# Chunk-causal hybrid encoder layer: GpSimd's head preparation, its low parts in four pieces, an operand on ScalarE

## The reference

```
h  = rmsnorm(x) * (1 + sc1) + sh1
z  = h @ w_in                         # q,k,v | shifted columns | gates
o_a = band attention (8 heads x 64)
o_b = RWKV-7: w_log, a, g, kk from z; S = S*w + sa (kk*a)^T + v k^T; y = S r; group norm; gate
merged = gates_a * (o_a @ w_out_attn) + gates_b * (o_b @ w_out_rwkv)
x  = x + gt1 * (merged @ w_out)       # "output stage" below
h2 = rmsnorm(x) * (1 + sc2) + sh2
x  = x + gt2 * ((silu(gg) * u) @ w_ffn_out),  u, gg = h2 @ w_ffn_in
y  = rmsnorm(x)
```

## Time and profile before

| what | value |
|---|---|
| timed runs | 1097.21 us median, 1095.9 to 1097.24 |
| profiled execution, span from the first to the last instruction | 1095.1 us (its own device time isn't listed apart; the median of the timed runs is 2.1 us above the span) |
| PE, matmuls | 1045.0 us busy (95%) |
| DVE | 395.5 us (36%) |
| ACT | 366.5 us (33%) |
| POOL | 368.7 us (34%) |
| mean granted TensorE clock | 0.980 |
| heads, about | 331 to 535 us |
| attention and RWKV output products, merge | 535 to 620 us |
| output stage | 620 to 674 us |
| feed-forward | 674 to 1085 us |

### The profile page before, as it was taken

The page is one execution under the profiler, slowest core; times in us unless marked ns, Lnnn a source line. Parts: engine busy times, 40 slices in busy tenths (PEclk is TensorE's granted clock), DMA queues, the critical chain, the costliest instruction groups (busy, mean ns, idle before and its releaser), DMA issues.

```text
span 1095.1 us, 25416 instructions
## 1 busy us (share of the span) xinstructions
PE 1045.0 (95%) x10988; PEld 966.9 (88%) x10988; DVE 395.5 (36%) x926; ACT 366.5 (33%) x745; POOL 368.7 (34%) x252
## 2 busy tenths in 40 slices
PE   6999999999998988989898999999999999999997
PEld 3899989999996766777787999999999999999997
DVE  4400000194045676566556576222222222200003
ACT  4443333353444444345232233322322232211112
POOL 2165433343316061401160333333343334344331
PEclk8899999999999999899998999999999999999999
DMA  9986666343311000020341532233222322132322
GB/s 358 352 276 235 234 206 198 99 139 119 113 42 36 18 7 22 13 82 3 131 130 43 198 116 58 77 92 99 77 77 83 107 78 65 55 104 79 92 67 82
DMA packets 118174, 122.23 MB, mean 112 GB/s; under 512 B 5396, under 2 KB 102848, under 8 KB 115656
## 3 DMA queue, kind: packets, MB, share of 16 engines
q1 hardware_dynamic: 112864, 111.86, 31.8%
q10 hardware_dynamic: 5224, 9.10, 2.5%
HBM read 108.33 MB, written 15.23 MB: 113 GB/s over the span
## 4 chain that ended last, share of the span: by engine, by line
PE 86%; DVE 7%; issue 3%; ACT 3%; POOL 1%; ACTq 1%; DVEq 0%; POOLq 0%
PE ps L1566 83%; PE ps L1917 2%; DVE s_sb L1306 1%; PE ps L1817 1%; POOL w_lo L595 1%; DVE s_sb L1340 1%; ACT x_sq L743 0%; DVE xn L1118 0%; DVE gring L1477 0%; DVE Pb L1277 0%; DVE y_sb L1549 0%; DVE mt L1479 0%; ACT mgh L1031 0%; DVE XX L1287 0%; ACTq L729 0%
## 5 line engine op out<-in xcount | busy, mean ns | idle before, releaser
L595 POOL TENSOR_TENSOR w_lo<-w_raw,w_hi 128x2048 fp32r<-128x2048 f32 (+1 forms) x66 | 282.3, 4277 | 564.0 <-ACT w_hi L753 544.9
L1566 PE MATMUL ps<-hh,w_hi 128*128 128x274 f32 x1376 | 290.0, 293 | 2.7 <-DVE hl L1128 2.0
L1566 PE MATMUL ps<-hh,w_lo 128*128 128x274 f32 x1376 | 288.1, 292 | 0.0
L1566 PE MATMUL ps<-hl,w_hi 128*128 128x274 f32 x1376 | 286.6, 291 | 0.0
L1566 PEld LDWEIGHTS ps<-hh,w_hi 128*128 128x128 f32 x1376 | 219.0, 190 | 12.8 <-issue 11.2
L1566 PEld LDWEIGHTS ps<-hh,w_lo 128*128 128x128 f32 x1376 | 218.7, 190 | 0.8 <-issue 0.8
L1566 PEld LDWEIGHTS ps<-hl,w_hi 128*128 128x128 f32 x1376 | 219.0, 190 | 0.0
L753 ACT ACTIVATE w_hi<-w_raw 128x2048 fp32r<-128x2048 f32 (+1 forms) x66 | 117.5, 1781 | 106.6 <-PE ps L1566 101.1
L1566 PE MATMUL ps<-ah,w_hi 128*128 128x274 f32 x352 | 75.3, 290 | 0.3 <-POOL w_lo L595 0.3
L1566 PE MATMUL ps<-ah,w_lo 128*128 128x274 f32 x352 | 75.4, 290 | 0.0
L1566 PE MATMUL ps<-al,w_hi 128*128 128x274 f32 x352 | 75.2, 290 | 0.0
(11 more groups left out here) (375 smaller groups left out, 1537.8 us busy)
## 6 DMA issues: line engine op xcount, KB each, us to landing
w_raw<-in_w_ffn_in SPq DMA_DIRECT2D x44, 512.0 KB, 4.6
w_raw<-in_w_in SPq DMA_DIRECT2D x42, 512.0 KB, 5.0
ada_l<-in_w_ada SPq DMA_DIRECT2D x16, 1024.0 KB, 6.4
ada_w<-in_w_ada SPq DMA_DIRECT2D x8, 1024.0 KB, 13.6
w_raw<-in_w_ffn_out SPq DMA_DIRECT2D x16, 384.0 KB, 4.0
w_raw<-in_w_ffn_out SPq DMA_DIRECT2D x16, 320.0 KB, 3.4
g_d<-gst SPq DMA_DIRECT2D x16, 274.0 KB, 2.4
gring<-g_d SPq DMA_DIRECT2D x16, 274.0 KB, 3.2
```

Source lines behind the costliest of these rows:

```text
L595: pool.tensor_tensor(w_lo[:, s, 0:cols], w_raw[:, s, 0:cols], w_hi[:, s, 0:cols].bitcast(F32), ALU.subtract).then_inc(lo_done, 1)
L1566: return pe.matmul(out, lhsT, rhs, start=start, stop=stop)
```

## The change

GpSimd: a new `low_in_four` subtracts 2048 columns in four instructions of 512 and raises `lo_done` with the last; it is used for `U_OB` and the four units of `w_out`, and the loop over the rest starts at `U_UP`. The preparation of pairs 1 to 3 also waits until the second tile of the pair before has its `XX + dg2` (`x0_done`), and `attn_low(hp - 2)` stands behind the preparation instead of ahead of it. ScalarE: the operand `tmp_a` of the output stage is made here in three instructions ahead of its rounding. VectorE: `mgl` of tile i - 1 is made after the products of tile i; the three operand instructions and two waits are gone.

```
@@ GpSimd
+            def low_in_four(i, s):
+                pool.wait_ge(hi_done, i + 1)
+                pool.wait_ge(unit_mm, i - 1)
+                for b in range(0, UC, UC // 4):
+                    ins = pool.tensor_tensor(w_lo[:, s, b:b + UC // 4], w_raw[:, s, b:b + UC // 4],
+                                             w_hi[:, s, b:b + UC // 4].bitcast(F32), ALU.subtract)
+                ins.then_inc(lo_done, 1)
...
             for hp in range(HP):
-                if hp >= 2:
-                    attn_low(hp - 2)
                 if hp:
                     pool.wait_ge(sc_mm, (hp - 1) * TT)
                     pool.wait_ge(gm_dve, (hp - 1) * TT)
+                    pool.wait_ge(x0_done, (hp - 1) * TT + 2)
                     for k in range(11):
                         prelude(pool, link, hp, k)
+                    if hp >= 2:
+                        attn_low(hp - 2)
...
-            low(U_OB, U_OB % 2)
+            low_in_four(U_OB, U_OB % 2)
...
-            two_by_two(pool, U_WO, NWO + NUP, low)
+            for i in range(U_WO, U_UP):
+                low_in_four(i, i % 2)
+            two_by_two(pool, U_UP, NUP, low)
@@ ScalarE, tile2(k)
+                a = tmp_a[:, k % 2, :]
+                act.wait_ge(pair_free, T_WO + k)
+                if k >= 2:
+                    act.wait_ge(h2_done, k - 1)
+                act.activation(a[:, 0:T], xT[:, k, 0:T], ACT.Copy, scale=gsc[:, 1, k, 0:1])
+                act.activation(a[:, S0:W], xT[:, k, S0:W], ACT.Copy, scale=gsc[:, 1, k, 1:2])
+                act.activation(a[:, T:T + 2], mod[:, SH2 + k, :], ACT.Copy).then_inc(h_f32, 1)
                 act.wait_ge(h_f32, k + 1)
-                act.activation(hh[:, k, :], tmp_a[:, k % 2, :], ACT.Copy).then_inc(hh_done, 1)
+                act.activation(hh[:, k, :], a, ACT.Copy).then_inc(hh_done, 1)
@@ VectorE
+            def merged_low(i):
+                dve.wait_ge(mgh_done, i + 1)
+                tt(mgl[:, i, :], mt1[:, i, :], mgh[:, i, :].bitcast(F32), ALU.subtract).then_inc(mg_done, 1)
             for i in range(KD):
...
-                dve.wait_ge(mgh_done, i + 1)
-                tt(mgl[:, i, :], mt1[:, i, :], mgh[:, i, :].bitcast(F32), ALU.subtract).then_inc(mg_done, 1)
+                if i:
+                    merged_low(i - 1)
+            merged_low(KD - 1)
...
                 a = tmp_a[:, j, :]
-                dve.wait_ge(pair_free, T_WO + k)
-                link(sts(a[:, 0:T], xT[:, k, 0:T], gsc[:, 1, k, 0:1], None, ALU.mult))
-                link(sts(a[:, S0:W], xT[:, k, S0:W], gsc[:, 1, k, 1:2], None, ALU.mult))
-                dve.tensor_copy(a[:, T:T + 2], mod[:, SH2 + k, :]).then_inc(h_f32, 1)
-                dve.wait_ge(h_f32, k + 1)
                 dve.wait_ge(hh_done, 2 * KD + k + 2)
```

## The result

The changed kernel takes 1086.2 us (median of five runs, 1083.7 to 1087.4) against 1097.1 us for the kernel before on the same chip (1095.9 to 1097.2). The ratio is 0.9906, with a 95% interval of 0.9889 to 0.9922. In a later comparison the same kernel took 1084.4 us against 1095.5, ratio 0.9903 (0.9880 to 0.9926).

A forecast was written before the change was run, and what follows sets the result against it. TensorE was taken as the bound, its matmul row filling 95% of the span. Merge 3.9, x_lo -0.1, operand 0 and heads 3.3 sum to 7.1 us, from 1097.2 to 1090.1 us; range 1087.0 to 1094.8.

The forecast's parts named there:

- What bounds, and where to look: Whole kernel: TensorE bounds it; time is lost at the merge and in the second and third head pairs.
- The low part in four: Merge: w_lo in four pieces adds 0 (-0.3 to +0.6); VectorE waits 1.15 us at most, not 3.6.
- Rival B: Merge: GpSimd keeps the port through its four pieces; gain 1.5 to 3.0, total about 1091.8; chance 0.08.
- The merge, 3.9: Merge, TensorE before tile 7: saves 2.4 us of waiting plus 1.3 and 0.2 of half clock.
- `x_lo` later, 0.1: Split at U_OB: x_lo starts later behind the pieces, costing 0.1 us (0 to +0.6).
- Operand, 0: Output stage: making the operand on ScalarE gains 0 and costs 0, as TensorE doesn't wait there.
- Rival E: Output stage: ScalarE becomes the bound; slower by 7.7 us, 1104.9; chance 0.04.
- The heads, 3.3: Head pairs, GpSimd's preparation waits: 1.7 from VectorE, 1.9 from the clock, -0.3 first pair; between -1 and +8.
- rival A: Heads: the s_sb scales take over the block, half clock stays; heads 0 to 1 us, total 1092.9; chance 0.17.
- rival C: Heads: the second and third pairs get all of the 8.0 us; total 1085.9 (up to 1087.5); chance 0.06.
- Rival D: Merge and heads: neither effect is the port's, both places only move; time within 0.2%; chance 0.08.
- The first pair's -0.3: First head pair: the preparation now runs against the scales, costing 0.3 us (bound -1).

The follow-up runs named there:

- e4_operand: Only the output-stage operand moved from VectorE to ScalarE, on the kernel before; 1096.4 us, ratio 1.000.
- e1_gate: Only GpSimd's new wait and the later place of attn_low, on the kernel before; 1087.8 us, ratio 0.9921.
- f1_fill_before: Kernel before plus nine spare 128x128 matmuls in TensorE's pauses in each pair's first round; 1091.3 us, ratio 0.9958.
- e8_both: Changed kernel with x_lo also in four pieces and the last attn_low waiting for the last pair's powers; 1083.5 us, ratio 0.9885.
- e2_pieces: Only the low parts of U_OB and w_out cut into four pieces, on the kernel before; 1092.7 us, ratio 0.9967.
- e3_defer: Only the deferred mgl, with w_lo in one instruction, on the kernel before; 1093.1 us, ratio 0.9977.
- f3_scales: Changed kernel, but the preparation of pairs 1 to 3 waits for the pair's first two s_sb scales; 1084.5 us, ratio 0.9903.

## Why the prediction was wrong, step by step

**What bounds, and where to look: right.** Both places named were the places where the time went.

**The low part in four: right.** VectorE waits for one piece (1.59 us at most, "no `mgl` over 2 us"). The Trainium skill, "SBUF — State Buffer", section "Who interferes with whom", has the port pair held for an instruction; the 4.90 us `mgl` under one long instruction and the 1.59 us under pieces agree. Rival B is out. It was drawn from the Trainium skill, "GPSIMD Engine Reference", section "Instruction dispatch", by which a core starts its next instruction when its share of the last is done; that no gap is left for VectorE was my inference: had GpSimd kept the port, the four pieces would have taken the 5.0 us that they take undisturbed, and not 6.85, with an `mgl` of 1.59 us among them. What was wrong is the "I add 0" for the cut itself: it costs 5.00 - 4.58 = 0.4 us, inside the bounds given; the time of the four gatings (4.89 us for 4 x 548) did not carry over to 4 x 512. The pieces end 18.2 us behind the merge's first `gring` (606.46 - 588.28), where 17.8 were foreseen (614.0 - 596.25).

**The merge, 3.9: right in mechanism, with a term that isn't fixed.** In the profiled run it is 36.74 - 32.60 = 4.14, and 0.5 more ahead of the first `gring` (46 matmuls in 8.95 us instead of 9.46; from 8.8 to 10.3 over these kernels, where a half clock falls in them). Of the 4.14, 2.6 are the wait (predicted 2.4) and 1.5 the clock (predicted 1.3 + 0.2). The second is paid in before and e4_operand, not in e1_gate and f1_fill_before. Credited to the deferral was a part that the pieces do alone.

**`x_lo` later, 0.1: 0.4.** That is the price of the cut ahead of it: `x_lo` ends 1.9 us after the first gating starts, 1.4 before. It lies within the bound of 0.6.

**Operand, 0: right**, in e4_operand as in the whole. Rival E is out.

**The heads, 3.3: the step that failed.** It was put as "of which I count half, 0.85" and "I take four tenths, 1.9", with 26.5 and 28 us from mask to `kcT` as the sign. Measured were 24.90 and 24.90: pairs 1 and 2 gained 8.4 us and not 3.6, all that they had over the last pair and a little more. Three terms were mis-sized.

- The immediate gain was 1.44 and 1.34 us by TensorE's pauses (an estimate, at most 3.5 for both), not 0.85 each. Halving VectorE's 1.7 had no row behind it, whereas TensorE's pauses, which I didn't add up, were there to read. And since "8.0 - 2 x 1.7" takes off the whole 1.7 per pair while only half was counted, 1.7 of the 8.0 us were booked nowhere.
- The 1.3 us per pair for scales of `s_sb` that meet the preparation didn't come: all scales together fell from 18.7 to 17.4 us, and the first two of pair 1 take 0.29 and 0.38 us, where they took 0.31 and 0.93. So the first `Pb` came 5.84 - 4.01 = 1.83 us earlier. With this rival A is out.
- The clock gave back the other some 5.6 us (at least 4.9), not 1.9: in 14 of 14 pairs with the wait it stays up, and in 10 of 10 with both blocks it falls, so a fraction in between fitted no single pair.

The last pair of before, taken as the mark, has 1.53 us of pauses itself (0.60, 0.45, 0.48), so that it wasn't the floor. The argument for rival C ("the last pair does it, with one blocked addition") was the better one and got 0.06. That its 1085.9 is only 0.3 off the result is in part luck: in the profiled execution the last pair took 2.9 us back, while 1.1 us came ahead of the heads, where the change does nothing, and 1.3 in pair 0, whose clock falls in some executions and not in others, with the wait and without it. The objection to it, that the last pair has no preparation, was wrong: behind the additions the preparation costs little, 24.90 us with it against 24.75 in the last pair of e8_both without. Rival D is out by e1_gate and e2_pieces, each of which gains at its own place.

**What the last pair took back.** In this execution 2.86 us were lost there again; that is no part of the change, since the second profile has 25.08. The first pair's -0.3 didn't come: at full clock it has 26.90 us after and 27.01 in e3_defer, with the ungated preparation.

**The sum again.** 2.6 to 4.1 (merge) - 0.4 + 0 + 8.4 = 10.6 to 12.1, with falls of the clock elsewhere to come off or on. Measured were 10.9 and 11.1. The range missed it because the heads' upper bound (+8), though named, was given to C alone instead of widening the low end.

## What to carry to other kernels

When a late vector instruction makes TensorE pause, add up TensorE's own pauses in the stretch; that is a first estimate of the immediate price, and a lowered clock behind it can bring it to twice or four times as much (1.3 to 1.4 us of pauses, 3.0 to 5.4 us per pair here). A fall of the clock comes or doesn't come at a place: compare places with and without it instead of taking a fraction, take a second profile before explaining a fall in a new place, and put the whole of it in the range. Hold a GpSimd job of some hundred columns back until the latency-bound instructions of VectorE are through, but not further: the next ones can be wider (f3_scales). Where it can't be held back, cut it, and expect the cut job to last a tenth to a half longer.

## What the hardware showed that I had not expected

- The same kernel, with the same instructions and blocks, had its clock at 0.50 in the last pair in one profile and at 1.00 in another: 27.97 against 25.08 us. Some 7 us at half clock cost 2.9 us there, so four tenths of the stretch.
- A wait of TensorE of the same 4.18 us was followed by half clock in two executions (114 matmuls in 16.3 us) and not in two others (14.8 us).
- Cutting a GpSimd instruction of 2048 columns into four unlinked ones costs 0.4 us where VectorE stays away (5.00 against 4.58), and 2.2 us where it gets in between (6.85 against 4.63; 6.64 in e2_pieces).
- In the first pair every kernel has the same pause of TensorE, 1.69 us, and the clock fell behind it in 9 of 15 profiles: 28.1 to 30.9 us from mask to `kcT` against 26.9 to 27.1. What decides it, which the kernels don't, stays open.
